# Attention: high and low halves of the transposed weights side by side, one 512-column product for both, and the reciprocals sent through the transposes' banks

## What is computed

```python
def dense_attention(q, k, v, sink):          # 8 query heads, 2 key heads, head width 64
    s = jnp.einsum('bqhgd,bkhd->bhgqk', qg, k) * (dh ** -0.5)
    if sink is not None: s = jnp.concatenate([s, s_sink], axis=-1)
    p = jax.nn.softmax(s, axis=-1)
    if sink is not None: p = p[..., :-1]
    return jnp.einsum('bhgqk,bkhd->bqhgd', p, v)

def window_attention(q, k, v, kc, vc, sink):
    # blocks of 128 queries against the block before, their own, the one after, and 256 context keys
    p = jax.nn.softmax(jnp.concatenate([s_loc, s_ctx, s_sink], axis=-1), axis=-1)
    return einsum(p_loc, vw) + einsum(p_ctx, vc)
```

## Time and profile before

| what | value |
|---|---|
| median of 3 runs | 4621.01 us (4619.41 to 4631.49) |
| the profiled execution | 4621.78 us, its span 4620.0 us |
| PE busy / DVE busy / ACT busy / POOL busy | 4249.3 / 2177.3 / 1573.8 / 900.7 us |
| the 16 units of at10, at11, at20, at21 | about 127, 127, 191 and 191 us |

### The profile page before, as it was taken

The page is one execution under the profiler, slowest core; times in us unless marked ns, Lnnn a source line. Parts: engine busy times, 40 slices in busy tenths (PEclk is TensorE's granted clock), DMA queues, the critical chain, the costliest instruction groups (busy, mean ns, idle before and its releaser), DMA issues.

```text
span 4620.0 us, 46359 instructions
## 1 busy us (share of the span) xinstructions
PE 4249.3 (92%) x18566; PEld 3097.0 (67%) x18566; DVE 2177.3 (47%) x3670; ACT 1573.8 (34%) x3044; POOL 900.7 (19%) x695
## 2 busy tenths in 40 slices
PE   7886889988999999988889999899989898999997
PEld 3446754757788888645457866565665677888886
DVE  2368844123556663336262327572655744333334
ACT  3566741132211111332332215353545633222222
POOL 2112225211434441016161000011000021000002
PEclk9998899999999999898979999999999999999999
DMA  5112242111334431311111210111000031111111
GB/s 196 51 58 92 82 150 87 28 64 64 105 105 116 117 114 48 109 56 46 55 46 55 78 45 22 34 63 54 14 23 19 19 128 32 51 46 55 46 39 62
DMA packets 257799, 308.89 MB, mean 67 GB/s; under 512 B 19072, under 2 KB 209936, under 8 KB 256304
## 3 DMA queue, kind: packets, MB, share of 16 engines
q1 hardware_dynamic: 238096, 227.15, 15.8%
q0 software_dynamic: 17408, 75.64, 5.2%
q10 hardware_dynamic: 2080, 3.15, 0.2%
HBM read 271.61 MB, written 34.28 MB: 66 GB/s over the span
## 4 chain that ended last, share of the span: by engine, by line
PE 63%; DVE 9%; ACT 5%; POOL 2%; issue 1%; DMA 0%; POOLq 0%; DVEq 0%; ACTq 0%
PE bank L194 61%; PE bank L197 2%; DVE Mx L214 1%; ACT at21P L203 1%; ACT at20P L203 1%; ACT Mx L203 1%; POOL sq L214 1%; DVE at21sm L232 1%; DVE at20sm L232 1%; DVE x L220 1%; DVE wfl L214 0%; DVE at20Pl L214 0%; DVE at21Pl L214 0%; DVE at11sm L232 0%; DVE at10sm L232 0%
## 5 line engine op out<-in xcount | busy, mean ns | idle before, releaser
L194 PE MATMUL bank<-h,wslot 128*128 128x512 f32 (+2 forms) x1616 | 682.9, 560 | 13.9 <-ACT h L203 3.8
L194 PE MATMUL bank<-hT,wslot 128*128 128x512 f32 (+3 forms) x1136 | 461.0, 562 | 13.9 <-DMA hT<-hspill 6.6
L194 PEld LDWEIGHTS bank<-h,wslot 128*128 128x128 f32 (+1 forms) x1616 | 288.1, 189 | 241.7 <-issue 225.6
L194 PEld LDWEIGHTS bank<-hT,wslot 128*128 128x128 f32 (+1 forms) x1136 | 211.7, 189 | 238.8 <-issue 232.3
L194 PE MATMUL bank<-ffn1h,wfh 128*128 128x512 f32 x704 | 279.8, 397 | 11.8 <-DVE ffn1l L220 10.9
L194 PE MATMUL bank<-ffn2h,wgh 128*128 128x512 f32 x704 | 276.3, 392 | 9.9 <-DVE ffn2l L220 9.5
L220 DVE SCALAR_TENSOR_TENSOR x<-bank,mod,x 128x512 f32<-128x512 f32 x224 | 164.3, 746 | 245.9 <-PE bank L194 245.4
L194 PE MATMUL bank<-ffn1l,wfh 128*128 128x512 f32 x704 | 274.9, 391 | 0.0
L194 PE MATMUL bank<-ffn2l,wgh 128*128 128x512 f32 x704 | 274.7, 390 | 0.0
L194 PE MATMUL bank<-ffn2h,wgl 128*128 128x512 f32 x704 | 274.6, 390 | 0.0
L194 PE MATMUL bank<-ffn1h,wfl 128*128 128x512 f32 x704 | 274.5, 390 | 0.0
(11 more groups left out here) (565 smaller groups left out, 9297.9 us busy)
## 6 DMA issues: line engine op xcount, KB each, us to landing
wslot<-in_w_in SPq DMA_DIRECT2D x40, 1024.0 KB, 5.5
ffn1t<-in_w_mod POOLq DMA_DIRECT2D x64, 512.0 KB, 4.8
wslot<-in_w_ffn_in SPq DMA_DIRECT2D x44, 512.0 KB, 5.2
Mx<-acsT SPq DMA_DIRECT2D x32, 512.0 KB, 4.8
at1w<-in_ada_w POOLq DMA_DIRECT2D x24, 512.0 KB, 4.7
wslot<-in_ffn_w_gate SPq DMA_DIRECT2D x22, 512.0 KB, 3.9
wslot<-in_ffn_w_up SPq DMA_DIRECT2D x22, 512.0 KB, 5.2
wslot<-in_w_ffn_out SPq DMA_DIRECT2D x20, 512.0 KB, 5.3
```

What stands on the lines that cost most here:

```text
L194: return Counted() if counting[0] else self.q.matmul(o, l, r, start=start, stop=stop)
```

## The change

The ring `PT` takes the place of `PTh` and `PTl`: each buffer of 1024 columns holds, for each of two key tiles, 256 columns of high half and then 256 of low half. A tile is then one product of 512 columns, with the result over all of bank 6: high times weights' high half on the left, times their low half on the right. Only rows 0 to 63 of the right half are used, so the product of the two low halves is left out of the sum. The r products no longer fit in bank 6: they take a bank of the ring `bt`, between the transposes, 128 partitions high, and ACT copies rows 64 to 127 to `rsx` at step 2 (`recip`). At the unit's end ACT makes two copies (rows 64 to 127 left, rows 0 to 63 right), DVE one addition, POOL the second, and DVE multiplies by the reciprocals from `rsx` one unit later, at step 1 (`out_y`).

```diff
             self.Pr = Ring([sb(f"{nm}P{i}", [640 if self.win else TT]) for i in range(4)])
-            self.PTh = Ring([sb(f"{nm}Ph{i}", [512], f32r) for i in range(4)])
-            self.PTl = Ring([sb(f"{nm}Pl{i}", [512], f32r) for i in range(4)])
+            self.PT = Ring([sb(f"{nm}Pt{i}", [1024], f32r) for i in range(4)])
...
+        def half(self, u, i, h):
+
+            na = min(2, len(self.segments(u[0])[1]) - i)
+            return self.PT[u, i][:, :].rearrange("p (a h n) -> p a h n", h=2, n=256)[:, 0:na, h, :]
+
+        def turned(self, u, i):
+            na = min(2, len(self.segments(u[0])[1]) - i)
+            return self.bt[u, i][:, 0:na * 256].rearrange("p (a n) -> p a n", n=256)
...
                 if i == 0:
+                    b = self.bt.take(u, "r")
+                    for ev in self.bt.freed(u, "r"):
+                        e.wait_ge(*ev)
+                    for x in range(2):
+                        e.wait_ge(*st.dve.after("rs", n, x0 + x))
+                        e.matmul(b[:, hs[x]], self.sm[n, x0 + x][:, 8:9].to_broadcast([128, 128]), ident).then_inc(st.pe("r", u, x), 1)
+                        self.sm.give((n, x0 + x), st.pe.now())
                     self.bo.take(u)
                     for ev in self.bo.freed(u):
                         e.wait_ge(*ev)
-                    for x in range(2):
-                        e.wait_ge(*st.dve.after("rs", n, x0 + x))
-                        e.matmul(self.bo[u,][0:64, 256 + x * 128:384 + x * 128], self.sm[n, x0 + x][:, 8:9].to_broadcast([128, 64]), ident).then_inc(st.pe("r", u, x), 1)
-                        self.sm.give((n, x0 + x), st.pe.now())
-                b = self.bo[u,]
-                ph, pl = self.PTh[u, i], self.PTl[u, i]
-                vhl, cs = self.at.vhl[self.g], tiles[i:i + 2]
+                vhl, pt = self.at.vhl[self.g], self.PT[u, i]
                 e.wait_ge(*st.act.after("ph", u, i))
-                for a, c in enumerate(cs):
-                    e.matmul(b[:, 0:256], vhl[:, c * 128:(c + 1) * 128], ph[:, a * 256:(a + 1) * 256], start=i + a == 0, stop=False)
                 e.wait_ge(*st.dve.after("pl", u, i))
-                for a, c in enumerate(cs):
-                    t = e.matmul(b[:, 0:256], vhl[:, c * 128:(c + 1) * 128], pl[:, a * 256:(a + 1) * 256], start=False, stop=i + a == len(tiles) - 1)
+                for a, c in enumerate(tiles[i:i + 2]):
+                    t = e.matmul(self.bo[u,][:, :], vhl[:, c * 128:(c + 1) * 128], pt[:, a * 512:(a + 1) * 512], start=i + a == 0, stop=i + a == len(tiles) - 1)
                 t.then_inc(st.pe("av", u, i), 1)
-                self.PTh.give((u, i), st.pe.now())
-                self.PTl.give((u, i), st.pe.now())
+                self.PT.give((u, i), st.pe.now())
...
+                e.tensor_tensor(self.half(u, i, 1), self.turned(u, i), self.half(u, i, 0).bitcast(f32), OP.subtract).then_inc(d("pl", u, i), 1)
                 self.bt.give((u, i), d.now())
 
             def fin(u):
+                o_ = self.ot[u,]
+                e.wait_ge(*st.act.after("o", u, 1))
+                e.tensor_tensor(o_[0:64, 0:256], self.bo[u,][0:64, 0:256], o_[0:64, 0:256], OP.add).then_inc(d("o", u), 1)
+                self.bo.give((u,), d.now())
+
+            def out_y(u):
                 n, x0 = u
-                o_ = self.ot[u,]
-                e.wait_ge(*st.act.after("o", u))
-                e.tensor_tensor(o_[0:64, 256:512], self.bo[u,][0:64, 0:256], o_[0:64, 0:256], OP.add).then_inc(d("o", u), 1)
-                e.wait_ge(*d.now())
-                m = self.g * 2 + x0 // 2
+                o_, m = self.ot[u,], self.g * 2 + x0 // 2
+                e.wait_ge(*st.pool.after("o", u))
+                e.wait_ge(*st.act.after("r", u))
                 for x in range(2):
-                    e.tensor_tensor(self.at.y[x * 64:x * 64 + 64, m * NL + n * 128:m * NL + (n + 1) * 128], o_[0:64, 256 + x * 128:384 + x * 128],
-                                    self.bo[u,][0:64, 256 + x * 128:384 + x * 128], OP.mult).then_inc(d("y", u, x), 1)
-                self.bo.give((u,), d.now())
+                    e.tensor_tensor(self.at.y[x * 64:x * 64 + 64, m * NL + n * 128:m * NL + (n + 1) * 128], o_[64:128, hs[x]],
+                                    o_[64:128, hs[2 + x]], OP.mult).then_inc(d("y", u, x), 1)
                 self.ot.give((u,), d.now())
-            self.walk(scores, soft, turn, lambda u, i: None, fin, lambda i, j: None)
+
+            def late(i, j):
+
+                if i and j == 1:
+                    out_y(self.units[i - 1])
+            self.walk(scores, soft, turn, lambda u, i: None, fin, late)
+            out_y(self.units[-1])
...
+                e.activation(self.half(u, i, 0), self.turned(u, i), AF.Copy).then_inc(a("ph", u, i), 1)
+
+            def recip(u, i):
+                if i:
+                    return
                 o_ = self.ot.take(u)
                 for ev in self.ot.freed(u):
                     e.wait_ge(*ev)
+                for x in range(2):
+                    e.wait_ge(*st.pe.after("r", u, x))
+                e.activation(o_[64:128, 256:512], self.bt[u, "r"][64:128, 0:256], AF.Copy).then_inc(a("r", u), 1)
+                self.bt.give((u, "r"), a.now())
+
+            def fin(u):
+                o_ = self.ot[u,]
                 nt = len(self.segments(u[0])[1])
                 e.wait_ge(*st.pe.after("av", u, (nt - 1) // 2 * 2))
-                e.activation(o_[0:64, 0:256], self.bo[u,][64:128, 0:256], AF.Copy).then_inc(a("o", u), 1)
-            self.walk(lambda n, x: None, soft, turn, lambda u, i: None, fin, lambda i, j: self.gate_act(e, i, j))
+                e.activation(o_[0:64, 0:256], self.bo[u,][64:128, 0:256], AF.Copy).then_inc(a("o", u, 0), 1)
+                e.activation(o_[0:64, 256:512], self.bo[u,][0:64, 256:512], AF.Copy).then_inc(a("o", u, 1), 1)
+            self.walk(lambda n, x: None, soft, turn, recip, fin, lambda i, j: self.gate_act(e, i, j))
+
+        def pool(self, e):
+
+            st = self.st
+            for u in self.units:
+                o_ = self.ot[u,]
+                e.wait_ge(*st.dve.after("o", u))
+                e.tensor_tensor(o_[64:128, 0:256], o_[0:64, 0:256], o_[0:64, 256:512], OP.add).then_inc(st.pool("o", u), 1)
 
     class Attention:
         def __init__(self, br, before):
@@ -3950,6 +3978,7 @@
             for gr in self.groups:
                 barrier(e, *gr.before)
                 gr.proj_pool(e)
+                gr.pool(e)
 
     att1 = Attention(1, [sz, mg0])
     drop(m1)
```

More of the change, by code:

```diff
@@ L3813, in turn @@
             def turn(u, i):
-                wd = min(2, len(self.segments(u[0])[1]) - i) * 256
-                pl = self.PTl.take(u, i)
-                for ev in self.PTl.freed(u, i):
-                    e.wait_ge(*ev)
                 e.wait_ge(*st.act.after("ph", u, i))
-                e.tensor_tensor(pl[:, 0:wd], self.bt[u, i][:, 0:wd], self.PTh[u, i][:, 0:wd].bitcast(f32), OP.subtract).then_inc(d("pl", u, i), 1)
+                e.tensor_tensor(self.half(u, i, 1), self.turned(u, i), self.half(u, i, 0).bitcast(f32), OP.subtract).then_inc(d("pl", u, i), 1)
                 self.bt.give((u, i), d.now())
             def fin(u):
-                n, x0 = u
-                o_ = self.ot[u,]
-                e.wait_ge(*st.act.after("o", u))
-                e.tensor_tensor(o_[0:64, 256:512], self.bo[u,][0:64, 0:256], o_[0:64, 0:256], OP.add).then_inc(d("o", u), 1)
-                e.wait_ge(*d.now())
-                m = self.g * 2 + x0 // 2
+                o_ = self.ot[u,]
[3 more added lines that the diff above has]
+            def out_y(u):
+                n, x0 = u
+                o_, m = self.ot[u,], self.g * 2 + x0 // 2
+                e.wait_ge(*st.pool.after("o", u))
+                e.wait_ge(*st.act.after("r", u))
                 for x in range(2):
-                    e.tensor_tensor(self.at.y[x * 64:x * 64 + 64, m * NL + n * 128:m * NL + (n + 1) * 128], o_[0:64, 256 + x * 128:384 + x * 128],
-                                    self.bo[u,][0:64, 256 + x * 128:384 + x * 128], OP.mult).then_inc(d("y", u, x), 1)
-                self.bo.give((u,), d.now())
+                    e.tensor_tensor(self.at.y[x * 64:x * 64 + 64, m * NL + n * 128:m * NL + (n + 1) * 128], o_[64:128, hs[x]],
+                                    o_[64:128, hs[2 + x]], OP.mult).then_inc(d("y", u, x), 1)
                 self.ot.give((u,), d.now())
-            self.walk(scores, soft, turn, lambda u, i: None, fin, lambda i, j: None)
+            def late(i, j):
[3 more added lines that the diff above has]
+            out_y(self.units[-1])
         def act(self, e):
@@ L3852, in turn @@
             def turn(u, i):
-                wd = min(2, len(self.segments(u[0])[1]) - i) * 256
-                ph = self.PTh.take(u, i)
-                for ev in self.PTh.freed(u, i):
+                self.PT.take(u, i)
+                for ev in self.PT.freed(u, i):
                     e.wait_ge(*ev)
```

(6 more changed lines are left out.)

## The result

The changed kernel takes 4742.24 us (median of 4 runs, 4739.48 to 4748.95), the kernel before 4621.35 (4 runs). The ratio is 1.026, 95% interval 1.0248 to 1.0273: slower by 121 us, where 105 were forecast.

The account below looks back on a forecast made before the run. It took unit A as bound by a TensorE, ACT and DVE chain without slack, B's end by TensorE's own work. Dense groups 68 plus window groups 37 gave 105 us on 4621.8: median 4726 us, range 4695 to 4758.

Parts of the forecast that it names:

- the merges: Stages right behind the attention that multiply `y` by the output weights; the forecast sum had no term for them.
- the end of each dense group: Last unit and end of a dense group: second copy, POOL's addition and handovers, about 2 us.
- The multiplications into `y`: DVE's two multiplications now stand ahead of the second low half: 0.59 us taken, bound 0 to 0.6.
- The r products behind the low half: They wait for the bank that the second low half frees: start at 3307.57 instead of 3305.80 in A.
- A: Dense unit kind bound by a chain through TensorE, ACT and DVE without slack; forecast 2.3 us longer.
- B: Dense unit kind with 0.96 us of slack on ACT's side; forecast 1.9 us longer, set by TensorE.
- The copy ahead of the exponentials: ACT's copy of the reciprocals precedes the first head's exponentials: 0.41 us with a handover; they start 2.3 us later.
- The three units without gate products, 6.9: Of four such units ending a dense group, three are followed by another and lengthen like A: 6.9 us.
- A window pair 2.6, the rest of such a group 3: Window attention: six pairs 15.7 us, last four units and group's end 3; a group 18.7, two 37.
- The width of the products: One 512-column product per tile run instead of two of 256: saving taken as 0, bound 5 us in all.
- The second rival: Only TensorE pays, the copy doesn't hold the exponentials: 78 us together, 4699 us; chance 10%.
- The third rival: TensorE's clock falls as units idle more: 30 us more if each of 60 pays 0.5, 4756 us; 13%.

Follow-up runs that it names:

- The first experiment: Changed kernel with DVE's two multiplications made late, at step 5 of the next unit instead of step 1: 4697.9 us, ratio 1.0163.
- the split: Changed kernel with the products of all key tiles but a unit's first and last made as two of 256 columns again: 4744.1 us, ratio 1.0258.
- the two moves: Changed kernel with the multiplications into `y` at step 5 of the next unit and the r products at step 1: 4641.7 us, ratio 1.0042.
- the late second copy: Kernel with the two moves, and ACT's second copy out of bank 6 behind the next unit's first high half: 4634.8 us, ratio 1.0026.
- the ends on DVE: Kernel with the late second copy, and both additions of each group's last unit on DVE: 4626.9 us, ratio 1.0011.
- The best version: Kernel with the ends on DVE, and the gate product issued behind a unit's third transposes instead of ahead: 4626.8 us, ratio 1.0009.
- the copy late: Changed kernel with ACT's copy of the reciprocals one step on, behind the first head's exponentials: 4718.2 us, ratio 1.0205.

## Why the prediction was right

Sign and cause were right, the size 16 us short (105 forecast, 121 measured; 119.5 of it in the six stages). The 16 are the window groups (7), the clock in the dense pairs (6.7) and the merges (4), less some 3 that the forecast had too much in the first pair and at the end of each dense group; the rest lies outside the six stages.

- **The multiplications into `y`, 0.59 us.** One takes 0.289 us (0.281), the pair 0.61; with the handovers on both sides the low half starts 1.13 us behind the negation instead of 0.38, so 0.75. Slightly short. The first experiment gave back 0.74 in each unit and 44 us in all.
- **The r products behind the low half.** They start 5.39 us after A's start (5.19 forecast) and 5.88 after B's (5.92). The first av product starts 0.47 us behind them for 0.58 before, so the 128-column weights have no price on TensorE; but ACT's copy starts 0.81 us behind them, where the forecast had 0.70.
- **The copy ahead of the exponentials.** 0.41 us, as forecast. The exponentials start 5.39 + 0.81 + 0.41 = 6.61 us after A's start instead of 6.30.
- **A 2.3, B 1.9.** At a clock of 1.00 A is 2.58 longer and B 1.62: a pair 4.20, the 4.2 of the forecast. That is luck, since two errors cancel: A's chain is the 0.3 above longer, and B's work behind the r products takes 8.49 instead of 8.74 us. The first pair of each group is only 2.8 and 3.1 longer, because its B is at a low clock in both kernels.
- **The three units without gate products, 6.9.** 14.21, 13.79 and 13.79 us against 11.84, 11.34 and 11.83: 6.8.
- **A window pair 2.6, the rest of such a group 3.** A pair is 2.8 longer (19.07 against 16.25). The last units and the end are the term that was mis-sized: the last four units of at10, up to the next stage, take 41.7 instead of 33.1 us, so 8.6 where one pair and the end had at most 5.6. Of the 8.6, 5.0 lie behind the very last transposes: 2.1 up to the next group's first products, with the longer row of copies and additions ahead of them, and 2.9 in these products, up to ACT's first instruction behind them. These products are the same in both kernels, and take 6.76 us at a clock of 0.56 instead of 3.81 at 1.00. Both kernels' timelines show it for the last unit's eight transposes, and the windows for the seventeen products (columns as in the earlier trace rows). The two window groups together: 44 us for 37.

```profile
2892.68 1.06 PE L197 MATMUL bank<-cst,at10P 128*128 128x128 f32 x8 [2.32 <-ACT at10P L203]
```

```profile
2911.22 1.94 PE L197 MATMUL bank<-cst,at10P 128*128 128x128 f32 x8 [1.53 <-ACT at10P L203]
```

```profile
2898.94:2902.75 3.81, 3.81 (x17) 3.31 (x18) 0.00 (x0) 0.00 (x0) 0.00 (x0) 1.00 0.00 0
2919.57:2926.33 6.76, 6.76 (x17) 5.42 (x18) 0.00 (x0) 0.00 (x1) 0.00 (x0) 0.56 0.00 0
```

- **Merges: nothing.** They were left out of the sum and took 4 us, at the lower clock shown above.
- **The width of the products: 0.** Confirmed by the split.
- **The second rival** (only TensorE pays, 4699) is out: ACT stands 38 us in at20 behind the r products, and moving the copy alone gave 24 us. But the copy was not the only way from the r products to the unit's end, which neither rival nor forecast saw.
- **The third rival** (the clock) came true in part, on top of the forecast. It costs 0.24 in an A and 1.44 in a B, twice in each dense group: 6.7 us. The first two units without gate products are at 0.88 too. What that costs is open: in the kernel with the split products the first of them takes 14.23 us at 1.00, as here 14.21 at 0.88, but with `y` late it takes 13.48 at 1.00 in at21 and 13.96 at 0.88 in at20. So part of the 6.8 above may be the clock's. With `y` late the pairs are back at 1.00, so the clock goes with the waits and is no cause of its own here.

So of 119.5 us in the six stages 71.4 are the dense groups' (42 for ten pairs of 4.2, 6 for the two first pairs, 13.6 for six units without gate products, 6.7 for the clock, 3 at the ends), 44 the window groups' and 4 the merges'. Undoing the two moves brings 101 back, the late second copy and the ends on DVE 15 more. The best version stands at 4626.8 us, 1.0009 of before, and doesn't beat it, since the 472 products that the change saves have no price that shows. Its dense groups are 2 us shorter each than before the change; at10 (+2.9) and the merges (+3.5 and +1.6) are what is left of the loss, and why the merges stay long is open.

## What to carry to other kernels

An operation that is put through a small ring of banks waits for the release of a bank that it has nothing to do with; look up who frees that slot, and at what point of the program. Steps of 0.4 to 0.8 us each, a few instructions apart, cost 2.6 us in a unit A when they came to lie between a result and the engine that waits for it. When one route of such a wait is cut and less comes back than it should, follow the same event down the other queues before doubting the theory.

## What was not expected of the hardware

- The granted clock fell in two A of each dense group and the B behind them, though the other A and B have the same instructions and, at full clock, the same waits (1.9 us in A, 2.3 in B). With waits of 1.1 us in A and 1.6 in B (`y` late) it fell in none of them but the group's first. With the copy late only B fell, two in each group, and no A, though its wait was 1.9 us as well. What singles these units out is open. The Trainium skill ("TensorE: Matmul & The Clock Gate", section "A second HAM failure mode: psum-queue depth-cycling") tells of a kernel that cycles through PSUM banks and whose clock goes up and down with the many short idles between groups of products; the trace agrees in kind, with 0.88 and 1.00 side by side.
- At the end of a group the granted clock is 0.50 to 0.61, and the merge's first sixteen products then take 7.1 to 10.0 us, with the same tiles.
- POOL adds 64x256 in 0.72 us (the forecast had taken half of 1.05), where 128x512 with four times the elements takes 1.05.
